# Order of the first 16 attention jobs in a hybrid attention and pooling layer: sorted by query half, or head by head in the order one, four, two, three steps

## What is computed

```python
z = h @ w_in                       # q, k, v, attention gate, pool input, pool gate: 3072 columns
s = einsum('bqhcd,bkhcd->bhcqk', q, k) * scale      # 4 heads, two 64-wide halves c each
a = softmax(where(causal, s, -inf))
o = (a[:, :, 0] - lam * a[:, :, 1]) @ v             # differential attention
attn = rms_norm(o, subln_g) * (1 - lam_init) * silu(g_attn)
pool = multiscale_pool(u, w_pool, pool_scale) * silu(g_pool)
h = layer_norm(ALPHA * h + concat(attn, pool) @ w_out)
h = h + (p @ w_pe) * sigmoid(h @ w_pg + b_pg)
```

## Time and profile before

| what | value |
|---|---|
| runs | 704.21, 706.76, 711.55 us, median 706.76 |
| time of the profiled execution | 704.96 us |
| its span, slowest core (core 1) | 703.4 us |
| spans of the cores | 697.6 to 703.4 us |
| attention steps 0 to 39 on core 1 | 137.0 to 272.5 us |
| block(5) after them | 272.5 to 292.3 us |

### The profile page before, as it was taken

One profiled execution on the slowest core, in us unless ns is written; L12 is line 12 of the kernel. 1 busy time (PEld: TensorE's weight loads), 2 busy tenths in 40 slices (PEclk: granted clock), 3 DMA queues, 4 the chain that ended last, 5 costly groups with the idle time before them and its releaser, 6 DMA issues.

```text
span 703.4 us, 10677 instructions; the slowest of 8 cores (697.6 to 703.4 us)
## 1 busy us (share of the span) xinstructions
PE 655.6 (93%) x4298; PEld 285.0 (41%) x4298; DVE 438.5 (62%) x799; ACT 432.8 (62%) x577; POOL 161.4 (23%) x156
## 2 busy tenths in 40 slices
PE   6998999988889987999999989999999899999995
PEld 2343444433334442444444434444444344444442
DVE  2129437268777788354544573767777776767884
ACT  2211322467868874587777872767777777777542
POOL 0568400000000000000000000134443444444442
PEclk9999999999999999999999999999999999999999
DMA  8999540120400000120344407601111111113203
GB/s 239 320 292 311 120 61 0 26 36 1 60 1 1 1 1 1 22 39 1 61 61 61 83 8 114 156 1 41 66 61 55 51 61 61 61 57 101 84 30 121
DMA packets 28386, 51.46 MB, mean 73 GB/s; under 512 B 3376, under 2 KB 12848, under 8 KB 28336
## 3 DMA queue, kind: packets, MB, share of 16 engines
q1 hardware_dynamic: 18656, 40.55, 18.5%
q0 software_dynamic: 9680, 10.22, 10.2%
HBM read 52.60 MB, written 8.39 MB: 87 GB/s over the span
## 4 chain that ended last, share of the span: by engine, by line
PE 70%; DVE 15%; ACT 5%; SPq 3%; DMA 3%; issue 2%; POOL 1%; DVEq 0%; ACTq 0%
PE psum_all L537 26%; PE psum_all L873 13%; PE psum_all L823 8%; PE psum_all L743 8%; PE psum_all L676 6%; PE psum_all L855 5%; SPq L154 3%; DVE sb_PT L839 2%; ACT sb_PT L829 2%; PE psum_all L779 1%; DMA sb_kT<-w_in 1%; DMA sb_Vt<-w_in 1%; DVE sb_Lhl L863 1%; DVE sb_arena L602 1%; PE psum_all L902 1%
## 5 line engine op out<-in xcount | busy, mean ns | idle before, releaser
L829 ACT ACTIVATE sb_PT<-psum_all 128x1024 bf16<-128x1024 f32 (+1 forms) x288 | 264.6, 970 | 72.7 <-PE psum_all L823 71.1
L537 PE MATMUL psum_all<-sb_xb,sb_wsec 128*128 128x512 bf16 x768 | 194.1, 389 | 16.7 <-DVE sb_arena L590 6.6
L873 PE MATMUL psum_all<-sb_PT,sb_Vt 128*128 128x512 bf16 (+1 forms) x576 | 142.6, 370 | 3.5 <-DVE sb_Vt L879 1.9
L537 PEld LDWEIGHTS psum_all<-sb_xb,sb_wsec 128*128 128x128 bf16 x768 | 71.7, 99 | 111.6 <-issue 26.7
L823 PE MATMUL psum_all<-sb_qT,sb_kT 64*128 64x256 bf16 (+1 forms) x1152 | 86.5, 266 | 1.9 <-DVE sb_mixT L627 1.5
L873 PEld LDWEIGHTS psum_all<-sb_PT,sb_Vt 128*128 128x128 bf16 x576 | 55.6, 99 | 67.0 <-DVE sb_Vt L879 2.3
L823 PEld LDWEIGHTS psum_all<-sb_qT,sb_kT 64*128 64x128 bf16 x1152 | 44.6, 94 | 67.1 <-issue 35.5
L855 PE MATMUL psum_all<-sb_PT,sb_ones_bf 128*32 128x512 bf16 (+1 forms) x576 | 60.4, 379 | 6.4 <-DVE sb_PT L839 5.0
L537 PE MATMUL psum_all<-sb_wsec,sb_xb 128*128 128x512 bf16 x256 | 65.8, 382 | 0.3 <-POOL sb_wsec L428 0.2
L676 PE MATMUL psum_all<-sb_wsec,sb_mixT 128*128 128x512 bf16 x256 | 63.0, 380 | 0.7 <-DVE sb_mixT L927 0.5
L743 PE MATMUL psum_all<-sb_wsec,sb_arena 128*128 128x512 bf16 x224 | 56.3, 380 | 2.6 <-DVE sb_arena L731 1.3
(11 more groups left out here) (166 smaller groups left out, 767.9 us busy)
## 6 DMA issues: line engine op xcount, KB each, us to landing
sb_Vt<-w_in SPq DMA_DIRECT2D x28, 256.0 KB, 8.9
sb_kT<-w_in SPq DMA_DIRECT2D x20, 256.0 KB, 10.2
sb_Vt<-xT SPq DMA_DIRECT2D x16, 256.0 KB, 12.4
sb_kT<-xT SPq DMA_DIRECT2D x16, 256.0 KB, 10.9
sb_xb<-xT POOLq DMA_DIRECT2D x4, 1024.0 KB, 10.9
sb_xb<-x_own SPq DMA_DIRECT2D x7, 512.0 KB, 3.5
out<-sb_xb SPq DMA_DIRECT2D x7, 512.0 KB, 2.7
sb_wsec<-w_out POOLq DMA_DIRECT2D x2, 1024.0 KB, 11.0
```

Source lines behind the costliest of these rows:

```text
L537: P.op(PE, lambda e: e.matmul(ps[:, bank, :], a, b, start=(kc == 0), stop=(kc == 7)), reads=[B_w[sec], wk[kc], bx, xk[kc]], writes=[B_bank ...
L829: P.op(ACT, lambda e, u=u, pi=pi, q0=q0: e.activation(out=PT[pi][:, :, :, q0:256].rearrange("p k c n -> p c k n"), in_=ps[:, 2 * u:2 * u + ...
L873: P.op(PE, lambda e, k=k, u=u, pi=pi, s=s, kb=kb, q0=q0: e.matmul(ps[:, BO, :].rearrange("p (c n) -> p c n", c=2)[:, :, q0:256], Vt[:, s * ...
```

## The change

Only the list of jobs of spans 0 and 1 is ordered in another way. The jobs, the steps in each, the fill and the later spans stay as they are.

```diff
         order = []
-        for hf in range(2):
-            for h in range(4):
-                order += [(0, hf, h), (1, hf, h)]
+        for h in range(4):
+            order += [(0, 0, h), (1, 1, h), (0, 1, h), (1, 0, h)]
         order += [(j, hf, h) for j in (2, 3) for hf in range(2) for h in range(4)]
```

## The result

| | before | after |
|---|---|---|
| median of the five fast runs | 706.76 us | 696.36 us |
| lowest run | 704.21 us | 695.62 us |
| profiled execution, its slowest core | 704.96, 703.4 us | 695.62, 694.0 us |
| region: first score matmul of step 1 to that of step 40, slowest core | 152.45 us | 141.8 us |

One further run of each kernel fell into a slower state of the chip (770.44 and 753.06 us), and the medians and the ratio leave it out. The ratio is 0.9867, interval 0.9841 to 0.9893: 1.3% faster, some 9.4 us. I had forecast 702.0 us (696.5 to 708), which is 4.8 us under the median before, and had given "within 1%" a chance of 0.73 and "faster by over 1%" one of 0.22. The direction was right. The gain is about twice the forecast one, and 2.5 times the 3.8 us that the sum gave against the profiled execution.

A forecast was written before the change was run, and what follows sets the result against it. PE, busy for 93% of the span, was taken to set the time, with its waits mostly on DVE. 704.96 - 3.1 (waits) - 0.7 (clock) = 701.2 us, or 703.0 against the median; forecast 702, range 696.5 to 708.

The forecast's parts named there:

- the sum: Profiled execution of 704.96 us less 3.1 us of waits and 0.7 us of clock, giving 701.2 us.
- Single-step jobs: PE's waits for the mask at steps 10, 20 and 30: 1.1, 1.1 and 1.8 us, sum 4.0.
- Shared banks: Steps 11, 21, 31 and 41, where `q_ss` and `q_sel` fall in one step: waits of 3.3 us, before 2.5 (1.7 + 0.8).
- Fill in a full bank: Fill opening in a bank still full, now at step 5 only: 0.9 us of wait, before 2.9.
- Pool chains: Steps 34 to block(5), two chains now ahead of a mask: waits of 5.4 us, before 6.7.
- Waits together: PE's waits from step 1 through block(5)'s start: 13.6 us against 16.7, a gain of 3.1.
- The clock: Half-rate stretches on the slowest core: between one fewer (-1.5 us) and none fewer (0), taken as 0.7 us gained.
- four clusters: Waits kept close together: 2.0 us at steps 10 and 11, 2.8 at 20/21, 2.4 at 30/31, 2.0 at 37.
- Rival 1: The slowest core loses all three half-rate stretches, 4.5 us besides the waits: 697.4 us; chance 0.2.
- Rival 2: Masks wait behind pool chains and the block still waits its 3.34 us: slower, 707.5 us; chance 0.18.
- Rival 3: Fill and DVE work only shifted, waits move and their sum stays: 704 to 706 us; chance 0.17.

The follow-up runs named there:

- the first experiment: The kernel before, with only block(5) beginning with bank 7 instead of bank 6; 700.61 us, ratio 0.9929.
- the version with less on DVE: Changed kernel with span 2 pool chains' first copy on ACT, their rest after the mask, and each mask ahead of the bank 4 copy; 693.77 us, ratio 0.9837.

## Why the prediction was right in kind and short in size

**Single-step jobs: two right, the third 0.5 too dear.** 1.1, 1.1 and 1.8 forecast; 1.12, 1.03, 1.28 measured. At step 30 DVE's queue from `fin_o` to the mask is as long as at step 4 (3.7 us both times, 230.91 to 234.62 and 148.59 to 152.29). But DVE begins it 0.53 us ahead of PE's `lsum` of the step before (231.44), where at step 4 it began 0.13 us behind it (148.46).

**Shared banks: right.** 3.3 forecast. Step 11 has 0.22 + 0.57, step 21 1.59 (1.7 forecast), step 31 0.57, step 41 0.35: 3.3. **Fill in a full bank:** 0.9 forecast, 0.79.

**Pool chains: right in mechanism, 0.6 too dear.** Forecast 5.4 us: 1.3, 2.0, 0.35, 1.0 and 0.8 at the block. The rows show 1.00, 1.56, none, 1.05 and 0.35. The first two cost 0.4 each more than their brackets, so the sum is 4.8. The block's second quantum didn't wait at all.

**Waits together:** forecast 13.6, shown 11.1 to step 40 and 11.5 with step 41. With the small gaps the gain is 6.1 us and not 3.1. I had walked the changed kernel more dearly than it came, by 2 us, and 0.6 us of the gain stands in no bracket.

**The clock: the step that failed.** "From one such stretch fewer on the slowest core (-1.5) down to none fewer (0) I take the middle, **0.7**." The slowest core lost all three, worth 4.5 us. The argument was that four clusters of 2.0 to 2.8 us are left, which would each keep their stretch. I took the sum over a step or two as what counts. The runs show that the clusters of steps 10, 11, 20, 21, 30 and 31, with the PE work between their waits, had no stretch on any core of the changed kernel; only the 1.56 us behind the chain had one, on four of eight. Over all kernels every stretch in this part stands at or right behind a wait of 1.5 us or more. From 1.5 to 1.9 us it went by the place: 1.77 at step 5 before four cores, 1.59 at step 16 five, 1.85 at step 37 none, 1.59 at step 21 now none. Waits of 2.04 and 2.10 at the block had one on three cores each, 2.93 on seven, 3.34 on five. The changed kernel has lost the three waits that had stretches behind them (1.77, 1.59 and 3.34) and got one new one that has (1.56). Rival 1, 697.4 us, was this case with the whole 4.5 us, and had been given 0.2; even it took the waits at 3.1 us, where 6.1 came.

The rule of the Trainium skill that a copy out of PSUM by DVE doesn't break PE's warmth ("TensorE: Matmul & The Clock Gate", "Loop structure matters more than you think") would have made this term 0. The page says it of matmuls that follow each other at once. The runs speak against taking it so where PE *waits* for that copy: with the bank of one quantum exchanged, stretches at the block went from five cores to none, and from none to three.

**Rival 2 fell.** Masks behind chains cost what they should, but the block doesn't wait on. The bank's turn decided it: 0.35 at the block, and 2.10 when the turn was put back. **Rival 3 fell** too.

**Against which base.** I had put the sum between the profiled execution and the median. Taken from profiled execution to profiled execution the gain is 9.3 us, from median to median 10.4; the ratio's interval holds both. Spans 2 and 3 didn't take quite what they took: the part behind the region is 0.5 us longer, for which no run was made.

What stays open: why one core has a stretch behind the same wait and another has none, and why the same length has one at one place and none at another. The 0.6 us that no bracket shows lie for the most part inside PE's rows: from start to start, without idle time, the region's matmuls take 130.5 us on core 7 of the first experiment, which has no stretch, and 130.0 on core 5 of the changed kernel. Which of them is open too.

## What to carry to other kernels

- When jobs are put in another order, list for each wait what stands in the queue of the engine waited for between the last thing PE got and the thing it needs. Done with durations of before, this gave the single waits of the changed kernel to within 0.5 us. For two other orders its sum was 1.9 and 3.7 us short (8.2 against 10.1, 12.3 against 16.0), by waits that the walk had left out.
- At each border of phases look at which bank the last fill of one and the first of the next use. With two banks in turn that is a matter of parity, an order far ahead flips it, and here it was worth 1.7 us of wait at each block, and 1.8 to 5.0 us of time with the clock.
- A long wait on PE may cost more than its length. Price it with the half-rate stretch behind it where the trace shows one behind waits of that size, and try several short waits in place of a long one; the pair run here shows fewer stretches for it, not yet a shorter time.

## What the runs showed of the hardware

- One wait of 2.9 us on DVE put PE at half rate on seven of eight cores; four waits of 0.3 to 0.6 us, with 4.1 us of cost in all, on none. At the places of these waits it was 10 stretches against none. Both kernels have the wait of 1.56 us at step 37 besides, with stretches on four cores and on one.
- Every stretch in this part, in all kernels, stands at or right behind a wait of 1.5 us or more; most such waits on most cores have none. The wait of 2.18 us at `block(7)` had one on 38 of 72 cores, and 0.46 us in its place on none of 16.
- A spell of half rate lost 1.7 us of clock each time, or double that; no other sizes were seen in this part of the kernel. In time it cost 1.5 us at steps 5 and 17 and 0.3 to 1.0 at step 37.
- The same wait of 1.59 us at step 21 had no stretch behind it on any core of the changed kernel, and one on three cores of the version with less on DVE.
- The cores run the same program with the same waits and differ in their stretches. Their spans lay 5.8 us apart before and 3.2 after. So a change that removes stretches gains more on the metric (9.4 us) than on the fastest core (697.6 to 690.8, 6.8 us).
